# Key pages turned on VectorE in 32x32 blocks, scores made by sixteen 32x32 tiles, and bias rows loaded through GpSimd's queue

## What is computed

```python
D_MODEL = 1024; SEQ = 256; DEC_BATCH = 8; DEC_SEQ = 8; PAST_LEN = 256; PAGE_SIZE = 128
MOBA_HEADS = 8; MOBA_HD = 128; MOBA_BLOCK = 256; MOBA_TOPK = 3
# cache_k, cache_v (N_PHYS, PAGE_SIZE, MOBA_HEADS, MOBA_HD); page_table (DEC_BATCH, 2)
x, state   = retention_layer(x, ...)                  # [q | k | v | gate], decay, w_out
k, v       = shared_kv(x, kv_norm_w, w_kv, k_norm_w)  # the new rows, k normed per head
q, g       = moba_query(x, norm_w, w_in, q_norm_w)    # q normed per head, * HD ** -0.5
k_seq      = concat(cache_k[page_table[b]], k_new[b]) # 256 past keys + 8 own keys
s          = q . k_seq + rel_bias[t5_bucket(q_pos - k_pos)]
y          = (softmax(s) @ v_seq) * silu(g) @ w_out + x
```

## Time and profile before

| | us |
|---|---|
| median of 3 runs | 509.38 |
| lowest, highest | 509.21, 510.33 |
| span of the profiled execution | 508.2 |
| TensorE busy | 502.0 |
| VectorE busy | 352.5 |
| ScalarE busy | 263.2 |
| GpSimd busy | 74.6 |

### The profile page before, as it was taken

The page is one execution under the profiler, slowest core; times in us unless marked ns, Lnnn a source line. Parts: engine busy times, 40 slices in busy tenths (PEclk is TensorE's granted clock), DMA queues, the critical chain, the costliest instruction groups (busy, mean ns, idle before and its releaser), DMA issues.

```text
span 508.2 us, 9171 instructions
## 1 busy us (share of the span) xinstructions
PE 502.0 (99%) x3401; PEld 434.0 (85%) x3401; DVE 352.5 (69%) x651; ACT 263.2 (52%) x532; POOL 74.6 (15%) x85
## 2 busy tenths in 40 slices
PE   7999999999999999999999999999999999999997
PEld 6989978899779978898899999977877778999885
DVE  3865539884789829893598978836756765676662
ACT  5836532574428633464652556945444655655630
POOL 0291004520082102720000240000000000000000
PEclk9999999999999999999999999999999999999999
DMA  8993969999899898999937976526797657684211
GB/s 256 333 349 118 275 245 313 376 358 231 284 343 386 235 277 283 354 328 230 264 103 277 334 244 256 188 83 238 249 326 238 216 171 242 226 309 154 83 53 52
DMA packets 79375, 125.49 MB, mean 247 GB/s; under 512 B 4051, under 2 KB 42148, under 8 KB 79204
## 3 DMA queue, kind: packets, MB, share of 16 engines
q1 hardware_dynamic: 79250, 124.89, 75.4%
q10 hardware_dynamic: 82, 0.02, 0.0%
HBM read 98.93 MB, written 27.57 MB: 249 GB/s over the span
## 4 chain that ended last, share of the span: by engine, by line
PE 95%; DVE 2%; DMA 1%; ACT 1%; issue 1%; SPq 0%; DVEq 0%; ACTq 0%
PE bank L884 45%; PE bank L881 20%; PE bank L865 7%; PE bank L1048 3%; PE bank L993 3%; PE bank L1061 2%; PE bank L1115 1%; PE bank L1007 1%; PE bank L940 1%; PE bank L1161 1%; PE bank L820 1%; PE bank L973 1%; PE bank L974 1%; PE bank L975 1%; DMA eye<-in_c_eye 1%; PE bank L961 1%
## 5 line engine op out<-in xcount | busy, mean ns | idle before, releaser
L1523 DVE TENSOR_TENSOR w_lo<-w_raw,w_hi 128x512 fp32r<-128x512 f32 x207 | 143.8, 733 | 65.7 <-ACT w_hi L1185 65.2
L1185 ACT ACTIVATE w_hi<-w_raw 128x512 fp32r<-128x512 f32 x208 | 118.4, 620 | 58.3 <-PE bank L884 35.0
L884 PE MATMUL bank<-xn_hi,w_hi 128*128 128x320 f32 x320 | 100.1, 317 | 0.7 <-ACT w_hi L1185 0.7
L884 PE MATMUL bank<-xn_hi,w_lo 128*128 128x320 f32 x320 | 97.7, 309 | 0.1
L884 PE MATMUL bank<-xn_lo,w_hi 128*128 128x320 f32 x320 | 97.6, 309 | 0.0
L881 PE MATMUL bank<-w_hi,xn_hi 128*128 128x512 f32 x160 | 65.0, 406 | 0.0
L884 PEld LDWEIGHTS bank<-xn_hi,w_hi 128*128 128x128 f32 x320 | 59.7, 188 | 4.7 <-issue 2.9
L881 PE MATMUL bank<-w_lo,xn_hi 128*128 128x512 f32 x160 | 62.6, 391 | 0.0
L881 PE MATMUL bank<-w_hi,xn_lo 128*128 128x512 f32 x160 | 62.5, 390 | 0.0
L884 PE MATMUL bank<-ym_hi,w_hi 128*128 128x320 f32 x192 | 60.9, 317 | 0.0
L884 PEld LDWEIGHTS bank<-xn_lo,w_hi 128*128 128x128 f32 x320 | 59.8, 188 | 0.4 <-DVE xn_lo L1572 0.2
(11 more groups left out here) (265 smaller groups left out, 766.5 us busy)
## 6 DMA issues: line engine op xcount, KB each, us to landing
w_raw<-in_ret_w_in SPq DMA_DIRECT2D x23, 1024.0 KB, 10.8
st<-in_state_ret SPq DMA_DIRECT2D x32, 512.0 KB, 8.4
out_ret_state_sample<-st SPq DMA_DIRECT2D x32, 512.0 KB, 4.6
w_raw<-in_ret_w_out SPq DMA_DIRECT2D x8, 1024.0 KB, 8.8
w_raw<-in_moba_w_in SPq DMA_DIRECT2D x8, 1024.0 KB, 6.1
cache<-in_cache_k SPq DMA_DIRECT2D x16, 512.0 KB, 4.9
w_raw<-in_w_kv SPq DMA_DIRECT2D x8, 1024.0 KB, 6.4
cache<-in_cache_v SPq DMA_DIRECT2D x16, 512.0 KB, 4.0
```

The costliest lines, as they stand in the source:

```text
L884: mm = pe.matmul(bank[out][:, 0:T], w[:, wk, P * tile:P * tile + P], x[:, k, :], **flags)
L1185: act.activation(w_hi[:, c % 2, part], w_raw[:, c % RAW, part], ACT.Copy).then_inc(w_hi_done, 1)
L1523: dve.tensor_tensor(w_lo[:, c % 2, part], w_raw[:, c % RAW, part], w_hi[:, c % 2, part].bitcast(F32), ALU.subtract).then_inc(w_lo_done, 1)
```

## The change

- **KP** becomes one VectorE instruction, which turns the page in 32x32 blocks from its buffer into `ktc` or, for every second page, into the scratch `ktc2`. TensorE, ScalarE and PSUM have no part in it. For this each key page is loaded by four DMAs of 128 KB on SP's queue instead of one of 512 KB, in an order of keys and features in which the blocks come out right, in pieces of 1 KB. There are six page buffers for the key pages, two of them in `mkT`.
- **KS** becomes 64 matmuls 32x32 by 128 keys, four partition groups of features by four groups of columns, summed in four banks (6, 3, 4, 5) in place of one; one KS takes half of two sequences' heads and pages: pages 2u and 2u+1 in the new order `key_page`.
- **SE** has two steps; each takes four banks out with four VectorE operations. The second half is kept in `late_ps`; SA has no such part left. SE 0 stands in slot 14, SE 1 in slot 25.
- The spreading of the queries goes from ScalarE to GpSimd: four copies of 32x64 for each head, each waiting for the one before, from `mqT`.
- `own_q` is a new layout of the queries for SN, made by GpSimd (a clearing of 128x1024 and two copies); SN has 32 matmuls.
- The bias rows come by 16 DMAs on GpSimd's queue behind that; `bn` follows in step QT.
- The slots: the pairs KP 0 and 1 go into the last mq chunk, KP 2 and 3 into slots 0 and 1, and further pairs into slots 5, 8, 11, 14, 18 and 20; KS 0 to 7 stand in slots 4, 7, 10, 13, 17, 19, 21 and 24; KX 0 to 3 in slots 15, 16, 26 and 27 (before: 16, 18, 26, 27). KX transposes 128 rows of the third tile, 64 of them zeros. The load of `tb` goes from KP 10 to KS 6.

```diff
-    for n in range(8):
-        at = 2 + 3 * n
-        if n:
-            g[at].append(("KS", n - 1))
-        if n == 4:
-            g[at].append(("SE",))
-        g[at] += [("KP", 2 * n), ("KP", 2 * n + 1)]
-    g[16].append(("KX", 0))
-    g[18].append(("KX", 1))
-    g[26].append(("KS", 7))
+    g[0].append(("KP", 2))
+    g[1].append(("KP", 3))
+    for u, at in enumerate((4, 7, 10, 13, 17, 19, 21, 24)):
+        g[at].append(("KS", u))
+        if u < 6:
+            g[at + 1] += [("KP", 2 * u + 4), ("KP", 2 * u + 5)]
+    g[14].insert(0, ("SE", 0))
+    g[25].append(("SE", 1))
+    g[15].append(("KX", 0))
+    g[16].append(("KX", 1))
...
# SP
-                sp.dma_start(cache[:, n % NCP, :], src[bass.ds(page, 1)].rearrange("o p h d -> p (o h d)"))\
-                    .then_inc(cache_loaded[n % NCP], 16)
+                src = a["cache_k"][bass.ds(page, 1)].rearrange("o (c i) h d -> i (o c) (h d)", i=32)
+                for g in range(4):
+                    sp.dma_start(page_at(n)[32 * g:32 * g + 32, :].rearrange("p (c x) -> p c x", c=4), src[:, :, 256 * g:256 * g + 256])\
+                        .then_inc(cache_loaded[page_slot(n)], 16)
...
-                elif kind == "ME" and step[1] == 5:
-                    sp.wait_ge(lines_stored, 64)
-                    for h in range(MH):
-                        r0 = 32 * (h % 4)
-                        sp.dma_start(bs[r0:r0 + 32, h // 4, :],
-                                     bass.AP(scratch.tensor, h * LINE + FAR - PAST, [[0, 4], [skew, NEW], [1, PAST + NEW]]))\
-                            .then_inc(bias_loaded, 16)
...
# TensorE
-                elif kind == "KP":
...
-                        mm = pe.transpose(bank[b][:, P * (h % 4):P * (h % 4) + P], cache[:, n % NCP, P * h:P * h + P], ident)
...
+                    u = step[1]
+                    q, pg = u // 2, u % 2
+                    pe.wait_ge(kt_done, 2 * u + 2)
+                    pe.wait_ge(wide_filled, MH)
+                    if u % 4 == 0:
+                        for b in PS_BANKS:
+                            await_free(pe, b, "PS", u // 4)
+                    for e in range(4):
+                        for s in range(2):
+                            at = 32 * (2 * s + q % 2) - NEW * (q % 2)
+                            for h in range(2):
+                                for g in range(4):
+                                    rows_at, c0 = slice(32 * g, 32 * g + 32), 32 * (2 * h + s)
+                                    keys_of = (ktc, ktc2)[s][rows_at, pg, 4 * h + e, :]
+                                    last[g] = pe.matmul(bank[PS_BANKS[g]][c0:c0 + 32, P * pg:P * pg + P],
+                                                        wide[rows_at, 8 * h + 2 * e + q // 2, at:at + 32], keys_of,
...
# VectorE
+                    await_page(dve, n)
+                    if n >= 4:
+                        await_ks(dve, n // 2 - 2)
+                    dve.transpose(keys_turned(n), page_at(n).rearrange("p (c x j) -> p x c j", c=4, j=32)).then_inc(kt_done, 1)
...
+                    half = step[1]
+                    dve.wait_ge(bias_loaded, 32 * MH)
+                    for b in PS_BANKS:
+                        await_full(dve, b, "PS", half)
+                    for x in range(2):
+                        for u in range(2):
+                            b, p = PS_BANKS[2 * u + x], 2 * half + u
+                            to = scores_at(p)[:, 0:PAST]
+                            dve.scalar_tensor_tensor(to, bank[b][:, 0:PAST], rsq[:, 16 + p:17 + p], to if x else bs[:, u, 0:PAST],
+                                                     ALU.mult, ALU.add).then_inc(bank_read[b], 1)
...
# GpSimd
+                for e in range(4):
+                    done.wait()
+                    ins = pool.tensor_copy(slots[32 * g:32 * g + 32, 8 * (h % 2) + 2 * e:8 * (h % 2) + 2 * e + 2, :, 16 * x:16 * x + NEW],
+                                           mqT[32 * e:32 * e + 32, h, TP:T].rearrange("p (n b t) -> p n b t", n=2, t=NEW))
...
+                    pool.wait_ge(lines_stored, 64)
+                    await_ret_over(pool)
+                    for h in range(MH):
+                        for s in range(2):
+                            r0 = 64 * (h % 2) + 32 * s + 16 * (h // 2 % 2)
+                            pool.dma_start(bs[r0:r0 + 16, h // 4, :],
+                                           bass.AP(scratch.tensor, h * LINE + FAR - PAST, [[0, 2], [skew, NEW], [1, PAST + NEW]]))\
+                                .then_inc(bias_loaded, 16)
```

237 lines of the change are left out of this document (128 added, 109 removed), and 2 rows, old and new, of the table banks.

## The result

| | before | after |
|---|---|---|
| median | 509.41 | 517.52 |
| lowest to highest, 4 runs each | 509.21 to 510.33 | 515.55 to 518.96 |
| profiled execution, its time and its span | span 508.2 | 518.96, span 517.0 |

The ratio is 1.0152, with an interval from 1.0127 to 1.0176. Forecast had been 505.9, faster, with a range from 499.5 to 512.5. The profiled execution is the longest of the four, 1.4 us above the median, so what follows counts out a difference of 8.8 us in the spans (517.0 against 508.2), where the medians differ by 8.1. The runs of the changed kernel also lie three times as far apart as those of the kernel before, 3.4 us against 1.1.

A forecast was written before the change was run, and what follows sets the result against it. TensorE, 95% of the chain, was taken to bound the kernel, with VectorE becoming the mk stage's bound. Span 508.2 - 12.2 + 8.3 + 0.4 = 504.7 us, plus about 1.2 gives 505.9, range 499.5 to 512.5.

The forecast's parts named there:

- What is taken off TensorE: Old KS with its pair of KP costs 2.90 us on TensorE's path; removing eight saves 23.2 us.
- What is put on TensorE: New KS at 1.3 us, eight times 10.4, plus 0.6 for SN; TensorE alone would gain 12.2 us.
- in these rows it is the columns that pace and not the count: Step pricing a new KS by eight rounds of 128 columns, 1.3 us, not by its 128 records.
- The bound from SN: If every record has its own price, SN's 0.018 us each makes a KS 2.5 us with entry and restart.
- What is put on VectorE: A page transpose takes 1.14 us, 0.54 more than the copy removed; VectorE becomes the bound of the mk stage.
- the hand-made list: VectorE's worked-out order in the mk stage, giving TensorE stalls of 4.0 us at KX 0 and 2.2 at KX 1.
- The smaller parts: ScalarE, mq stage, SP loads, SA and bias loads: only the mq stage was charged, 0.4 us.
- the rival that carried the chance of "slower": Bias rows on GpSimd's queue come late and delay SE 0; 514.7 us at 2.0 us a load; chance 0.11.
- GpSimd beside VectorE in mq: GpSimd's 32 copies beside a VectorE busy for 85% of the mq stage: 0.4 us, between nothing and 2.
- a slow KS: Rival: every record of KS has its price, a KS costs 4.2 us, time about 520; chance 0.05.
- The clock, named among what would make the forecast wrong: Sign: TensorE's clock falling in the idle 4 us at KX 0; each 4 us so spent costs 2 more.
- 8.3 forecast as given back: TensorE's stalls on VectorE in the mk stage: 0.5 + 4.0 + 2.2 + 1.4 + 0.2 us.

The follow-up runs named there:

- half_turn: Changed kernel with twelve of the sixteen VectorE transposes (from KP 4 on) over 512 elements instead of 1024: 514.32 us, ratio 1.0085.
- half_all: Changed kernel with half of each KS, half of the transposes from KP 4 on, and pages from the seventh on read at one row in 32: 506.59 us.
- half_all_pool: As half_all, but the loads of key pages 10 to 15 are issued by GpSimd's queue instead of SP's: 500.27 us, ratio 0.981.
- small_pages: Changed kernel with the last six key pages (loads 10 to 15) read at one row in 32: 510.56 us, ratio 1.0017.
- before_pad: Kernel before, with only KX changed to turn 128 rows of the third token tile, 64 of them zeros: 508.85 us, ratio 0.998.

## Why the prediction was wrong, point by point

**What is taken off TensorE**, 23.2 us: right. Chunk 36, which has no stall in it, takes 10.6 us where 10.2 had been worked out, the difference being a dearer KS.

**What is put on TensorE**, 1.3 us for a KS: mis-sized. It measured 1.92 and 0.10, 5.8 us more over eight. The first step that failed is "in these rows it is the columns that pace and not the count". With sixteen tiles in a round, about half of the round's time does not go with its columns: half as many columns made a KS 0.42 us shorter, not half as long. The bound from SN, 2.5, was on the right side. Of the two rules of the Trainium skill, TensorE: Matmul & The Clock Gate, that were quoted, the floor of 25 ns between starts ("Wait — 56ns, not 53.3ns?") agrees with a tile that follows itself, 27 ns in the kernel cut one tile after itself, and does not hold for tiles in turn, 14 ns in the new KS. The other rule, some 4 ns for each further tile ("Measured speedup vs the span model"), is short of the 7.7 ns for each record that the two widths give.

**What is put on VectorE**, 1.14 us a page: 1.17 from start to start (343.13 to 344.30 in the trace), right. With half of the elements (half_turn) it is 0.64 (342.64 to 343.28), so a further element costs about 1.04 ns, as good as the 1.055 that the prediction had taken from L1523 and L1797; here the trace agrees with the rule of the Trainium skill that it quoted from Vector Engine (DVE) Microarchitecture Reference, 3.8. That VectorE becomes the bound of the stage was right too, though the changed kernel hides it: there TensorE is late itself and waits only 1.5 and 2.3 us at KX 0 and KX 1. With half of KS it waits 3.3 and 2.1 us there, and SE 0's first operation starts at 360.93 and the copy for KX 0 is done at 365.4, where the hand-made list had 361.5 and 365.9 for a stage that begins 0.3 us later. The second half of the list was off: for SE 1 it had a wait of 1.4 us and that run has 3.0, since a page was late.

**The smaller parts.** Bias loads: 0.63 us each to issue, landed 5.0 to 8.9 us later, `bn` made at 354.4, nobody waits for them but GpSimd itself; the rival that carried the chance of "slower" did not happen, and with the loads back on SP nothing changed. GpSimd beside VectorE in mq: 0.4 us forecast, nothing measured; matmul by matmul the two kernels run in step from 262 to 331. The transposes of KX, left at nothing, became 0.9 us cheaper. SP's loads, "about 1.5 us more each" and "waited for by no one", were right for the changed kernel: 2.6 us a page against 1.1 for one load, TensorE never waits for weights in the stage, and ScalarE once, for 1.4 us. The 6.3 us between half_all and half_all_pool are no measure of them, since there the one-row loads take longer to issue. The traffic of these loads was not weighed at all: the same bytes in pieces of 1 KB and in a shorter stage, a DMA share of 1.15 from 338 to 350.

**What was missing altogether** is the supply of instructions. This is the second step that failed, and the dearer one: by the prediction, what is taken off TensorE "shortens the kernel for as long as nobody else becomes late", which leaves out that TensorE may have no instruction to execute. The list of rivals had prices for a slow KS and for VectorE, and none for an engine that has nothing to execute. The rows to see it by were there: the page of before lists 27 instruction packets of 16 KB, and the new KS's 256 instructions were counted in the prediction, but as matmuls. It cost 7.9 us inside two KS, 5.8 of them idle. The clock, named among what would make the forecast wrong, fell after the waits in KS and at KX 1; it is the rest of the 7.9, about 2 us, and about 3.5 us more outside of KS.

In sum: 12.2 forecast for TensorE alone, 7.5 measured (23.2 - 16.2 - 0.4 + 0.9); 8.3 forecast as given back, 16.3 measured (4.9 + 7.9 + 3.5). The two parts can't simply be taken off one by one: with nearly all of the issue idle time gone (small_pages) the kernel is still not faster than before, 1.0017.

## What to carry to other kernels

Count the instructions of a burst as a resource of its own: eight bursts of 256 in under 2 us each made TensorE run dry in some of them, also with the page loads of the kernel before, and eight of the same number over 3.5 us did not. Full DMA engines made it worse in KS 4. When a stage is made shorter, ask what else has to fit into it, its loads, the queue that issues them in order, and the engine with the second highest load; here several limits lay within 10 us of each other, and taking away one of them gave at most 7 us, another none. And look at what a cut-down experiment does besides what it is for: a load of one row in 32 moves fewer bytes, and its four parts took 3.1 us to issue where the whole ones took 1.8.

## What the hardware showed that had not been expected

- TensorE stops inside a run of matmuls, without any semaphore, for 2.6 and 3.2 us in the changed kernel and for 0.25 to 4.5 in all 38 cases, always at a step of 256 of its instructions, and goes on 2.3 to 3.0 us after a 16 KB instruction packet starts. The idle times move from one KS to another between schedules, and the times of such kernels spread by 1.5 to 7.4 us where the kernel before has 1.1 to 2.7.
- Sixteen 32x32 tiles in turn start 14 ns apart at 128 columns and 11 at 64; four column tiles of 32 columns in turn 10 ns; one tile after itself 27 ns.
- After idle times of 2.6 and 3.2 us in KS 2 and KS 4, and after those at KX 0 and KX 1 close to each other, the granted clock was at its lower level; it does not follow every such time: with the KS in two slots it stayed at 1.00 through a wait of 2.2 at KX 1 and an issue idle time of 2.0, in the profiled execution.
- Six transposes in a row of which two have 64 rows cost TensorE 0.23 us more (0.80) than with these padded by zeros to 128 rows (0.57, before_pad).
- SP issues the four loads of a key page in 1.81 us when they are read whole, and in 3.12 when each takes one row in 32.
